# A two-block network on one core: the root of two RMS norms moved from the operand to the finished product

## The reference

```python
def rms_norm(x, w):
    y = xf * lax.rsqrt(jnp.mean(xf * xf, axis=-1, keepdims=True) + EPS)
    return (y * w.astype(jnp.float32)).astype(x.dtype)

    u = rms_norm(h, norm_mix_w[l])
    proj = u @ w_in[l]
    xa, ga, qb, fb, ib, gb = jnp.split(proj, split_at, axis=-1)
...
    h = h + jnp.concatenate([ya, yb], axis=-1) @ w_out[l]
    gate = jax.nn.sigmoid(rms_norm(h, ple_norm_w[l]) @ w_ple_gate[l] + b_ple_gate[l])
    h = h + gate * (p[l] @ w_ple_proj[l])
```

## Time and profile before

| | |
|---|---|
| median of 3 runs | 2764.44 us (2760.41 to 2765.36) |
| the profiled execution | 2766.62 us, its span 2764.8 us |
| mean granted TensorE clock | 0.963 |
| busy share | PE 90%, PEld 71%, DVE 56%, ACT 42%, POOL 29% |
| first layer | 0 to 207 us, its tiles from 25 us |
| output product, gate | 207 to 267 us, 267 to 347 us |
| all that is behind them (second block) | 347 to 2765 us |

### The profile page before, as it was taken

How to read it: one execution, slowest core, us unless ns; L and a number is a source line. 1 busy time by engine, 2 the same in 40 slices (tenths; PEclk the granted TensorE clock), 3 DMA queues, 4 the chain that set the end, 5 groups by cost and what they waited for, 6 DMA issues and landing times. The chain is left out here.

```text
span 2764.8 us, 66158 instructions
## 1 busy us (share of the span) xinstructions
PE 2476.3 (90%) x28416; PEld 1973.8 (71%) x28416; DVE 1554.5 (56%) x2508; ACT 1159.9 (42%) x1947; POOL 790.2 (29%) x501
## 2 busy tenths in 40 slices
PE   7998999999799995788888888789999999998997
PEld 5776677778577785677777776668788788775665
DVE  5634489953851413565665664343552299825974
ACT  4633331152444432554555554234432366622233
POOL 2422201422222225554454651110000033141132
PEclk9998999999899997999999999899999999999998
DMA  4213354434326442111111100542532200144431
GB/s 154 84 61 130 130 156 120 120 107 155 122 99 221 165 163 73 38 49 38 55 48 34 55 21 15 204 164 79 172 100 69 91 1 1 63 136 139 142 107 61
DMA packets 90287, 272.66 MB, mean 99 GB/s; under 512 B 13584, under 2 KB 14608, under 8 KB 89872
## 3 DMA queue, kind: packets, MB, share of 16 engines
q1 hardware_dynamic: 73104, 229.28, 25.9%
q10 hardware_dynamic: 16896, 39.16, 4.0%
HBM read 203.04 MB, written 36.70 MB: 87 GB/s over the span
## 5 line engine op out<-in xcount | busy, mean ns | idle before, releaser
L375 PE MATMUL ps<-h_parts_conv,w_parts_one 128*128 128x512 f32 x3168 | 581.1, 342 | 28.1 <-DVE h_parts_conv L361 20.6
L375 PEld LDWEIGHTS ps<-h_parts_conv,w_parts_one 128*128 128x128 f32 x3168 | 489.4, 189 | 122.5 <-issue 27.1
L375 PE MATMUL ps<-scratch_scan 64*64 64x64 f32 (+1 forms) x16704 | 386.6, 235 | 100.1 <-issue 53.6
L375 PEld LDWEIGHTS ps<-scratch_scan 64*64 64x64 f32 x16704 | 345.6, 137 | 148.5 <-issue 109.1
L372 ACT ACTIVATE scratch_scan<-ps 128x384 f32<-128x384 f32 (+1 forms) x656 | 264.2, 461 | 317.7 <-PE ps L375 187.0
L443 POOL TENSOR_TENSOR w_parts_one<-ring,w_parts_one 128x1024 fp32r<-128x1024 f32 x83 | 206.0, 2484 | 575.3 <-ACT w_parts_one L372 575.1
L375 PE MATMUL ps<-h_parts_attn,w_parts_rwkv_out 128*128 128x512 f32 (+1 forms) x1536 | 327.9, 372 | 3.6 <-DVE h_parts_attn L369 3.6
L375 PEld LDWEIGHTS ps<-h_parts_attn,w_parts_rwkv_out 128*128 128x128 f32 x1536 | 262.9, 189 | 62.0 <-issue 8.4
L369 DVE SCALAR_TENSOR_TENSOR scratch_conv<-scratch_conv,vec 128x512 f32<-128x512 f32 (+1 forms) x408 | 257.5, 700 | 0.2
L372 ACT ACTIVATE w_parts_rwkv_out<-ring 128x1024 fp32r<-128x1024 f32 x104 | 109.6, 1056 | 343.2 <-PE ps L375 327.5
L375 PE MATMUL ps<-h_parts_block,w_parts_one 128*128 128x512 f32 x960 | 236.8, 405 | 8.1 <-DVE h_parts_block L361 6.0
(11 more groups left out here) (222 smaller groups left out, 3385.7 us busy)
## 6 DMA issues: line engine op xcount, KB each, us to landing
ring<-in_weights SPq DMA_DIRECT2D x311, 512.0 KB, 3.7
rwkv_spill<-scratch_conv ACTq DMA_DIRECT2D x64, 384.0 KB, 2.3
stream<-rwkv_spill SPq DMA_DIRECT2D x64, 384.0 KB, 3.6
scratch_conv<-scratch_conv SPq DMA_DIRECT2D x120, 103.1 KB, 2.2
scratch_conv<-scratch_conv SPq DMA_DIRECT2D x120, 67.4 KB, 2.0
x_spill<-stream ACTq DMA_DIRECT2D x16, 384.0 KB, 2.5
kept_gate<-scratch_attn ACTq DMA_DIRECT2D x64, 64.0 KB, 2.6
y_spill<-scratch_scan SPq DMA_DIRECT2D x8, 384.0 KB, 2.5
```

The source lines that it names most:

```text
L375: return nc.tensor.matmul(o, l, r, start=start, stop=stop)
```

## The change

The scaling by the root leaves the operand. ACT rounds `X` times the norm weight in one step (`scale=` of an ACT copy), DVE takes the low part in one step from the same product, so neither waits for the root. The root goes into `R1` in SBUF, and DVE multiplies each finished tile by it in its PSUM bank (`rescale`), ahead of ACT's eviction, which now waits for `rescaled`. That is done for the 24 tiles of the first layer and the 8 of the gate.

With it several things move. The first weight block is the first DMA, the stream comes in pieces of 2, 2 and 4 tiles, the constants behind weight block 1, the context and the ring behind it behind the root. The squares of the first layer stand behind the rounding of the stream, their sum is made by DVE (`S.add`) and one product of ones inside tile 1 (`behind`). `small_vectors` moves on DVE from ahead of all to behind rescale 4, its Exps on ACT into step 5, two small Silus into step 16. DVE's steps of the first layer are the same, with a rescale between them at given places. In the gate the total of squares stands ahead of the tiles and the root behind the highs; the first projections stand behind tiles 1 and 2, the total of the context's squares behind tile 2.

The steps are those of before; rescale 12 stands ahead of the last recurrence. The diff, cut to its core:

```diff
@@ first layer @@
             def _(sp):
+                R.supply(sp, RINGT, weights, 1)
                 sp.dma_start(VEC, vectors).then_inc(loads, 16)
-                sp.dma_start(X[:, 0:2, 0:TX], xs[:, 0:2]).then_inc(x_in[0], 16)
-                sp.dma_start(CON, consts).then_inc(x_in[1], 16)
-                for q in range(1, 4):
-                    sp.dma_start(X[:, 2 * q:2 * q + 2, 0:TX], xs[:, 2 * q:2 * q + 2]).then_inc(x_in[q], 16)
+                for q, (a, b) in enumerate(X_PIECES):
+                    sp.dma_start(X[:, a:b, 0:TX], xs[:, a:b]).then_inc(x_in[q], 16)
+                R.supply(sp, RINGT, weights, 2)
+                sp.dma_start(CON, consts).then_inc(consts_in, 16)
                 R.supply(sp, RINGT, weights, SLOTS)
-                sp.wait_ge(e_asked, 1)
-                sp.wait_ge(e_ready, 2)
+                sp.wait_ge(e_ready, 1)
                 sp.dma_start(X[:, :, TX:TT], ctxT.rearrange("(k p) t -> p k t", p=P)).then_inc(loads, 16)
...
-                    tile_product(pe, bank(n % 2), TX, fresh=(split_low, base_low, 1) if n == 0 else None)
+                    tile_product(pe, bank(n % 2), TX, fresh=(split_low, base_low, 1) if n == 0 else None,
+                                 behind=(4, total) if n == 1 else None)
...
+                def rescale(n):
+                    v.wait_ge(blocks_done, PSTART["in1"] + n + 1)
+                    vtt(bank(n % 2), bank(n % 2), R1).then_inc(rescaled, 1)
...
+                for k in range(DT):
+                    v.wait_ge(in_hi, base_hi + k + 1)
+                    stt(PARTS["H"][:, 1, k, :], X[:, k, 0:TX], V("norm_mix_w", k), PARTS["H"][:, 0, k, :].bitcast(F32),
+                        ALU.mult, ALU.subtract).then_inc(split_low, 1)
+                for m in range(1, DT):
+                    S.add(v, m)
+                v.wait_ge(e_ready, 1)
+                for m in range(4):
+                    rescale(m)
+                    conv(m)
+                rescale(4)
+                small_vectors()
+                for n in range(5, 9):
+                    rescale(n)
+                v.wait_ge(gates_done, 8)
+                gate_input(0)
+                gate_input(1)
+                rescale(9)
+                gate_input(2)
+                gate_input(3)
+                rescale(10)
+                recurrence(0)
+                rescale(11)
+                recurrence(1)
+                recurrence(2)
+                rescale(12)
+                recurrence(3)
+                decay_sums(0)
+                decay_sums(1)
+                rescale(13)
+                decay_sums(2)
+                decay_sums(3)
+                rescale(14)
+                chunk_rest(0)
+                chunk_rest(1)
+                rescale(15)
+                chunk_rest(2)
+                chunk_rest(3)
+                keep_values(0)
+                keep_values(1)
+                rescale(16)
...
+                round_block(a, 1)
                 a.wait_ge(loads, 16)
+                for q, (first, end) in enumerate(X_PIECES):
+                    a.wait_ge(x_in[q], 16)
+                    for k in range(first, end):
+                        act(PARTS["H"][:, 0, k, :], X[:, k, 0:TX], ACT.Copy, scale=V("norm_mix_w", k)).then_inc(in_hi, 1)
+                round_block(a, 2)
+                for m in range(DT):
+                    S.square(a, m)
...
+                    if n == 5:
+                        a.wait_ge(e_asked, 1)
+                        act(TINY[:, 56:60], t1, ACT.Exp, scale=-1.0).then_inc(e_ready, 1)
+                        act(TINY[:, 60:68], TINY[:, 48:56], ACT.Exp).then_inc(e_ready, 1)
...
-                    a.wait_ge(blocks_done, PSTART["in1"] + n + 1)
+                    a.wait_ge(rescaled, n + 1)
@@ gate @@
+                S_MIX.total(pe)
                 for m in range(DT):
...
-                    if m < 2:
-                        projected(m)
-                    if 1 <= m < DT - 1:
+                    if m in (1, 2):
+                        projected(2 * m - 2)
+                        projected(2 * m - 1)
+                    if 3 <= m < DT - 1:
                         projected(m + 1)
...
-                    act(PARTS["H"][:, 0, k, :], H[:, k, :], ACT.Copy).then_inc(in_hi, 1)
+                    act(PARTS["H"][:, 0, k, :], X[:, k, 0:TX], ACT.Copy, scale=V("ple_norm_w", k)).then_inc(in_hi, 1)
+                a.wait_ge(sq_used, S_MIX.base + DT)
+                alink(act(R1, RSTD[:, 0:TX], ACT.Ln, scale=1.0 / D, bias=EPSC[EPS]))
+                act(R1, R1, ACT.Exp, scale=-0.5).then_inc(e_ready, 1)
...
-                    a.wait_ge(blocks_done, PSTART["gate1"] + m + 1)
+                    a.wait_ge(rescaled, 24 + m + 1)
...
+                    p = PS[:, (m % 2) * 512:(m % 2) * 512 + 512]
+                    v.wait_ge(blocks_done, PSTART["gate1"] + m + 1)
+                    vtt(p, p, R1).then_inc(rescaled, 1)
```

132 lines of the change are left out of this document (58 added, 74 removed).

## The result

The changed kernel took 2773.75 us in the median of six runs (2764.69 to 2780.42), the kernel before 2765.71 in the median of six. One of those six took 4038.36 us; the ratio is taken from the undisturbed (fast) runs alone. It is 1.0036, with a 95% interval of 1.0021 to 1.0052: some 10 us slower by the ratio, 8.0 by the medians, where +3.7 was forecast. The median lies inside the stated range (2758.5 to 2775.0); the call, "no measurable difference" as the likeliest, was wrong. Two later comparisons gave 1.0033 (1.0020 to 1.0046) and 1.0022 (1.0010 to 1.0034). The mean of the three ratios is 1.0030, or 8.4 us; the three differences of medians are 8.0, 9.0 and 6.0 us.

The account below looks back on a forecast made before the run. TensorE, busy 90% of the span, was taken as the bound, so its stops near the changed places counted. -9.9 + 6.3 + 7.8 - 0.5 = +3.7 us gave a median of 2768 us, range 2758.5 to 2775.

Parts of the forecast that it names:

- no measurable difference: The call for the whole kernel: its time stays the same within what a measurement can tell; chance 0.46.
- The start: First layer's front, to tile 3's end: TensorE starts at about 8.6 us and tile 3 ends at 40.5; gain 9.9 us.
- it and the block behind it land by 24.1 + 3.5 + 1024/370 = 30.4: First layer's front: context load, issued at 24.1 us, and the next ring block land in time for a part needed at 35.
- The small vectors: First layer, behind rescale 4: the moved chain delays rescale 5 and the gate sigmoid, so TensorE stops 4.8 us; loss 6.3 us.
- The walk: Following the engines' queues step by step with the profile's durations; it gave +7.8 us for the rescales.
- The rescales: First layer: 24 rescales on DVE, 0.7 us each, hidden except between tiles 9 and 17; loss 7.8 us.
- The gate: Gate stage: tile 3 starts at 297.1 instead of 298.36 us, the last rescale costs 0.75 unhidden; gain 0.5 us.
- at the low level as before: Gate stage: the first tile starts at 271.42 us as before and again runs at the low clock, 7.39 us for 24.
- (a): Rival, faster: rescales fall into DVE's gaps, tile 2 runs fast, DVE isn't held in the small vectors; 2759 us, chance 0.18.
- part 3: The prediction's term for the first layer's 24 rescales on DVE: +7.8 us, between +2 and +11.
- (b): Rival, slower: POOL's parts hold rescales too, three of them (9, 11, 17) by 2.4 us each; 2775 us, chance 0.18.
- (c): Rival at the start: block 0 and the stream land late despite the order, tile 3 ends near 45; 2773 us, chance 0.12.

Follow-up runs that it names:

- e5: On e1: the context load issued behind two more ring blocks and no longer behind the root; ratio 0.9998 to the kernel before.
- e17: The change of the first layer alone, with the gate stage as in the kernel before; ratio 1.0038 to the kernel before.
- e18: The changed kernel run a third time with nothing altered, with its own trace; ratio 1.0022 to the kernel before.
- e10: The changed kernel run a second time with nothing altered, with its own trace; ratio 1.0033 to the kernel before.
- e4: The kernel before with only the gate stage's change, its first layer as before; ratio 0.9999 to the kernel before.
- e11: The changed kernel with rescale 5 moved on DVE ahead of the small vectors; median 2766.71 us, ratio 1.0009 to the kernel before.
- e7: On e1: tiles 12 to 15 evicted without the root, which DVE's copy of the turned values puts on; ratio 1.0001 to the kernel before.
- e8: On e1: context behind two more blocks, squares first, values with the turned root, each rescale one convolution earlier; ratio 0.9980 to the kernel before.
- e1: The changed kernel with the small vectors' first five steps ahead of DVE's low halves, the Exps ahead of ACT's high halves; ratio 0.9995 to the kernel before.

## Why the prediction was right and wrong

**The start: -9.9, measured -8.8, then -7.4.** The order of events was the forecast one, each a little late: TensorE at 9.21 (8.6), root 25.3 (24.1), tile 2 at 28.84 (27.7). The first 1.1 us are the root's: the sums were put at seven steps of 0.7 behind POOL's part, and took 6.72 us, the first of them 1.95. The step that failed behind that is "it and the block behind it land by 24.1 + 3.5 + 1024/370 = 30.4": the block landed at 32.1, and what waited for it first was not tile 3 but ACT, with the eviction of tile 1 and the convolutions behind it, so a gate sigmoid, and TensorE 1.13 us at 50.08. I had followed the block to the part and not to what is queued behind the rounding on ACT, nor to which convolution would meet a part. e5 priced it at 1.5 us. The stop itself isn't in every execution: in e17 and e18 tiles 2 and 3 took 14.23 and 14.00 us, the convolutions met the parts otherwise (the third starts at 39.31 in e18, at 41.68 in the first trace), TensorE didn't stop there, and tile 5 ended at 57.1 and 57.0.

**The small vectors: +6.3, measured +7.3 in one trace and 6.5 to 6.6 in two others.** The walk was right to 0.2 us where it could be checked: chain finished at +9.6 (67.0), TensorE on at +12.2 (12.0), a stop of 4.81 (4.8). What the low level costs was put at 1.6 (the sum of 4.8 and 1.6 is 6.4, not 6.3). It took 1.45 at the gate products (tile 7 starts 2.77 us behind them instead of 1.32), and reached into tile 7, for 0.9 us in this trace and 0.1 to 0.2 in e10 and e18. The row of that microsecond has PEclk 0.50 behind POOL, the level of 1.2 GHz, after a stop of 4.81 us:

```profile
72.00:73.00 1.00, 1.00 (x3) 0.34 (x1) 0.00 (x0) 0.52 (x1) 1.00 (x1) 0.50 0.00 0
75.00:76.00 1.00, 1.00 (x6) 0.82 (x5) 0.00 (x0) 0.00 (x0) 0.00 (x0) 1.00 0.60 246
```

The Trainium skill (ScalarE: Activation LUTs, What ACT_TABLE_LOAD costs) has a drain of about 1380 ns with each switch of tables. It isn't there in the changed kernel either: the load of 58.72 starts as the rounding ends (58.71), and 60.01 follows 58.72 + 1.28. So the sum without it stands.

**The rescales: +7.8, measured +5.2, with the extra 0.9 of the low level in tile 7 in the term before.** From tile 7's end (79.33): rescale 10 ends at 21.5 (forecast 22.1), the first root is used at 24.2 (24.6), recurrences 0 to 2 and rescale 12 end at 33.7 (34.4), tile 14 starts at 35.4 (36.1), tile 15 at 44.9 (45.8), tile 18 ends at 71.2 (73.7). The walk ran 0.9 us too slow by tile 15. The rest is a stop before tile 17 of 0.98 instead of 2, and the half price of a low level behind it, which didn't come: tile 17 took 5.75. Not forecast were small stops before tiles 12 and 13 (0.29 and 1.23); tile 15 came 0.9 earlier than forecast in spite of them.

**The gate: -0.5.** In size it holds (e4: 0.9999; at 696 it is 0.8 early in all and 0.4 late if the 1.2 of its first layer are taken off). The step "at the low level as before" was wrong: in the first trace and in e4 the first tile ran at full speed and brought 1.7 us, in e10 and e18 only 0.7 to 0.9, and the end of the stage took most of them back, with a rescale, a sigmoid and a longer wait for the sums (5.47 against 4.33), where I had written 0.75.

**The sum.** Up to 696 us it is +4.0 to +4.7 against +3.7 forecast. That it comes so near is in part luck: the start brought 2.5 us less than forecast and the rescales cost 2.6 less, and the two cancel. The rivals fell as mechanisms: (a), since DVE was late and not idle (its sum also took +1 for the rescales, where part 3 had +2 as its least); (b), since the rescales took 0.70 us on the mean (32 of them, 22.2 us in all), the one at 91.76 in the middle of a part. By the rule of the Trainium skill (SBUF — State Buffer, SBUF: two separate sides) the pair of ports is locked by steps with two SBUF inputs or in a 2-port mode, and a rescale has one such input; the trace agrees, 0.70 against 2.17 for the next step. The number of inputs alone doesn't tell: a step from SBUF to SBUF with one tile as input was held too, 2.18 us at 26.79 (before a part was done at 28.69), against 0.55 at 41.68. No run shows the mode. (c) was right in one point, a block that lands late, for 1.5 us and not for 5.

**What made the forecast wrong** is the last step of the sum: "On the profiled execution (2766.62, span 2764.8) that is 2770.3; this execution lies 2.2 over the median of the three times shown". It carries the +3.7 of the two stages to the end and puts what comes behind them, 347 to 2765 us, at nothing. The runs show +4.4 at 696 us and +8.4 by the mean ratio (1.0030). So some 4 us come in behind the point where the programs are the same again; none of the eighteen runs accounts for them, and their cause stays open. The bound for "slower" was 5.5 us: by the shift at 696 alone the call would have held, by a hair. A sum of +3.7 with terms that proved good to 2.6 us was no ground for 0.46 on "the same" against 0.38 on "slower".

## What to carry to other kernels

A step queued behind a long chain on one engine is late by the whole chain: before an order is written, ask of each eviction what stands ahead of it, and put the chain behind the eviction. One moved line (e11) gave 6.4 us at tile 7 and 6.1 in the medians. To put a scale on a result instead of on an operand shortens the start, but makes an engine's step stand between a product and its eviction for every tile; here that was free only where DVE was idle at the tile's end. A load that isn't needed soon goes behind the blocks that are. And a sum of shifts read from the front of one trace is not yet a forecast of the median: here 4 us of 8 came in where nothing had been changed.

## What the runs showed of the hardware

- The tiny steps of the chain (128 x 4) are held by a part of POOL like large ones: 2.36 us for one at 51.59, 0.16 for the next.
- Stops of nearly the same length had different sequels: after 3.34 us tile 15 took 7.38, after 3.33 in e5 7.08, in e7 after 3.93 even 8.55 (in e8 after 3.94 7.31); after 1.23 and 0.98 us tiles took 5.75. And tile 2 behind 2.82 us took 5.75 in e1, while in the changed kernel tiles 2 and 3 together took 12.89 instead of 11.5.
- Fewer steps on DVE didn't make DVE earlier (e7): what it met of POOL's parts changed with them.
